# Modulation slabs in rounded pieces, with roots and forget sums made ahead of the local attentions

## What is computed

```python
q, k = rms_norm(q_heads, q_gain), rms_norm(k_heads, k_gain)   # fox and moba, heads of 64
c = cumsum(log_sigmoid(f + f_bias))                           # fox alone: forget sums
s = q @ k.T * d ** -0.5 + c[:, None] - c[None, :]             # then a causal softmax, times v
# moba: q and k are turned by a partial rope instead; no forget sums
...
# second block, needed there long after: a condition c and one for the context
mod_lat = jax.nn.silu(c) @ w_mod + b_mod                      # 1024 x 6144
mod_ctx = jax.nn.silu(c_ctx) @ w_mod + b_mod
```

## Time and profile before

| | us |
|---|---|
| Median of 3 runs (lowest, highest) | 2408.41 (2407.76, 2408.49) |
| The profiled execution's own time | 2396.61 |
| Its span in the profile | 2394.8 |
| Attention stage of layer 0, of layer 1 | 117.95, 117.95 |

### The profile page before, as it was taken

How to read it: one execution, slowest core, us unless ns; L and a number is a source line. 1 busy time by engine, 2 the same in 40 slices (tenths; PEclk the granted TensorE clock), 3 DMA queues, 4 the chain that set the end, 5 groups by cost and what they waited for, 6 DMA issues and landing times. The chain is left out here.

```text
span 2394.8 us, 41799 instructions
## 1 busy us (share of the span) xinstructions
PE 2197.3 (92%) x17910; PEld 1977.9 (83%) x17910; DVE 1003.1 (42%) x2016; ACT 1159.0 (48%) x1663; POOL 1205.6 (50%) x308
## 2 busy tenths in 40 slices
PE   8999989899999999889899999888978777998998
PEld 7999865489999999865488999766857777998998
DVE  2332754424222222565334221376656777333551
ACT  5544532466345434632356443555874554554443
POOL 6776610075878877630074876432310000675785
PEclk9999999899999999999999999898998988999999
DMA  7555422253556555431243655321213111553553
GB/s 258 169 170 171 154 72 89 70 176 123 194 171 200 185 176 180 141 123 64 97 141 111 199 180 172 114 70 53 72 58 103 37 34 40 192 170 127 176 179 115
DMA packets 304102, 319.02 MB, mean 133 GB/s; under 512 B 7897, under 2 KB 295117, under 8 KB 303405
## 3 DMA queue, kind: packets, MB, share of 16 engines
q1 hardware_dynamic: 303917, 316.34, 41.3%
HBM read 313.10 MB, written 3.21 MB: 132 GB/s over the span
## 5 line engine op out<-in xcount | busy, mean ns | idle before, releaser
L558 POOL TENSOR_TENSOR slab_lo<-ring,slab_hi 128x2048 fp32r<-128x2048 f32 (+2 forms) x188 | 843.5, 4499 | 560.0 <-ACT slab_hi L549 560.0
L549 ACT CAST slab_hi<-ring 128x2048 fp32r<-128x2048 f32 (+2 forms) x188 | 347.6, 1851 | 412.6 <-PE bank L449 284.9
L444 PE MATMUL bank<-x_parts_hi,slab_hi 128*128 128x256 f32 x1760 | 436.4, 286 | 0.5 <-ACT slab_hi L549 0.5
L445 PE MATMUL bank<-x_parts_lo,slab_hi 128*128 128x256 f32 x1760 | 431.6, 283 | 0.0
L444 PEld LDWEIGHTS bank<-x_parts_hi,slab_hi 128*128 128x128 f32 x1760 | 337.4, 192 | 3.8 <-issue 2.6
L445 PEld LDWEIGHTS bank<-x_parts_lo,slab_hi 128*128 128x128 f32 x1760 | 337.5, 192 | 1.2 <-issue 1.0
L379 POOL TENSOR_TENSOR slab_lo<-ring,slab_hi 128x2048 fp32r<-128x2048 f32 (+1 forms) x54 | 243.7, 4538 | 127.4 <-ACT slab_hi L368 91.9
L449 PE MATMUL bank<-x_parts_hi,slab_lo 128*128 128x256 f32 x1760 | 247.8, 283 | 7.8 <-POOL slab_lo L558 7.8
L449 PEld LDWEIGHTS bank<-x_parts_hi,slab_lo 128*128 128x128 f32 x1760 | 226.9, 192 | 9.4 <-POOL slab_lo L558 9.4
L411 PE MATMUL bank<-hidden_hi,slab_hi 128*128 128x256 f32 x704 | 194.4, 276 | 0.0
L412 PE MATMUL bank<-hidden_lo,slab_hi 128*128 128x256 f32 x704 | 194.3, 276 | 0.0
(11 more groups left out here) (659 smaller groups left out, 4972.2 us busy)
## 6 DMA issues: line engine op xcount, KB each, us to landing
ring<-in_ffn_w_in SPq DMA_DIRECT2D x88, 1024.0 KB, 5.1
ring<-in_ffn_w_out SPq DMA_DIRECT2D x32, 1024.0 KB, 5.1
ring<-in_w_in SPq DMA_DIRECT2D x27, 1024.0 KB, 5.3
ring<-in_mix_w_in SPq DMA_DIRECT2D x24, 1024.0 KB, 5.3
ring<-in_w_mod SPq DMA_DIRECT2D x24, 1024.0 KB, 5.1
ring<-in_w_up SPq DMA_DIRECT2D x22, 1024.0 KB, 5.1
ring<-in_ffn_w_out SPq DMA_DIRECT2D x16, 768.0 KB, 4.4
ring<-in_mix_w_out SPq DMA_DIRECT2D x8, 1024.0 KB, 5.2
```

Source lines behind the costliest of these rows:

```text
L444: pe.matmul(out, w[0][:, k, col], act[0][:, k, :], start=(k == 0), stop=False)
L445: pe.matmul(out, w[0][:, k, col], act[1][:, k, :], start=False, stop=False)
L549: act.copy(self.hi[p][:, 0:w], K.ring[n % RING][:, 0:w]).then_inc(self.hi_ready, 1)
L558: pool.tensor_tensor(self.lo[p][:, 0:w], place[:, 0:w], self.hi[p][:, 0:w].bitcast(F32), ALU.subtract)\
```

## The change

In the attention stage a modulation slab is taken in four pieces (128 partitions by two groups of 256). ACT rounds a piece (`act_round`), DVE makes its remainder (`dve_rest`), and PE multiplies both with four columns: the two conditions' rounded parts and their remainders (`c`). Four rows come out instead of two, and the last turn adds them with a selector (`sel`). There are three places for pieces. PE takes a piece at two of the loop's three calls a step, 36 in 18 steps, and none ahead of the loop. Squares, head sums and roots for q and k move into the inverse stage (`LocalRoots`), with one of the first three slabs ahead of them; the forget sums move into the projection (`ForgetSums`). The scan runs two steps ahead of the loop instead of four, the state's memset and first answer come behind the normed tiles on DVE, and the two rotations stand before the scan's second step.

```diff
@@ project_stage, act @@
                 last.then_inc(lora_read, 1)
+                act.wait_ge(forget_in, 1)
+                act.activation(forget.e, forget.e, ACT.Exp).then_inc(forget_exp, 1)
                 evacuate(12)
@@ project_stage, dve @@
+                own.after(dve, last)
+                forget.dve_bounded(dve, s["f"], col("f_bias")).then_inc(forget_in, 1)
                 heads(11)
+                dve.wait_ge(forget_exp, 1)
+                forget.dve_sums(dve)
                 heads(12)
+class ForgetSums:
...
+    def dve_bounded(self, dve, f, bias):
+        self.K.dve_own.after(dve, dve.tensor_scalar(self.x, f[:, :], bias[0:4, :], None, ALU.add))
+        return dve.scalar_tensor_tensor(self.e, self.x, -1.0, self.x, ALU.mult, ALU.min)
+    def dve_sums(self, dve):
+        own.after(dve, softplus_small(dve, own, self.e, self.s, self.s2, self.q, self.s))
...
+class LocalRoots:
+    BANK = 4
...
+    def act_squares(self, act):
+        for i in range(4):
+            act.activation(self.sq[:, 2 * i:2 * i + 2, :], self.qk[:, 2 * i:2 * i + 2, :], ACT.Square).then_inc(self.squared, 1)
+    def pe(self, pe):
+        for i in range(4):
+            pe.wait_ge(self.squared, i + 1)
+            pe.matmul(self.K.bank[self.BANK + i][:, :], self.K.c("headsum"),
...
+    def act_roots(self, act):
+        for i in range(4):
+            act.wait_ge(self.summed, i + 1)
+            last = act.activation(self.sq[:, 2 * i:2 * i + 2, :], K.bank[self.BANK + i][:, :].rearrange("p (a t) -> p a t", a=2),
+                                  ACT.Ln, bias=K.c("eps"), scale=1.0 / 64)
+            last.then_inc(self.logged, 1)
+        act.wait_ge(self.logged, 4)
+        act.activation(self.sq[:, :, :], self.sq[:, :, :], ACT.Exp, scale=-0.5)
@@ rwkv_stage @@
+                    pe.wait_ge(intra_read, 9)
+                    mod.pe_first(pe, 0, 1)
                     pe.wait_ge(intra_read, 16)
-                    mod.pe_first(pe)
+                    roots.pe(pe)
+                    mod.pe_first(pe, 1, mod.FIRST)
+                    roots.pe_free(pe)
                     inv.pe(pe)
...
-                    inv.act(act, between=lambda i: mod.act_first(act) if i == 1 else None)
+                    roots.act_squares(act)
+                    for g in range(4):
+                        inv.diagonal(act, g)
+                    roots.act_roots(act)
+                    inv.act(act, between=lambda i: mod.act_first(act) if i == 1 else None, first=4)
@@ Modulations @@
-    AT_A_CALL = 2
-    AHEAD = 8
+    CHUNKS = 4
+    PLACES = 3
...
+    def dve_c(self, dve):
+        dve.tensor_tensor(self.sel[:, :], K.c("ident", slice(0, 4), n=2), K.c("ident", slice(0, 4), first=2, n=2), ALU.add)
+        dve.wait_ge(self.c_hi, 1)
+        dve.tensor_tensor(self.c[:, :, 2:4], K.cs[:, :, :], self.c[:, :, 0:2].bitcast(F32), ALU.subtract).then_inc(self.c_lo, 1)
...
+    def act_round(self, act, upto):
+        for j in range(self.rounded, min(upto, self.end)):
+            n = self.n0 + self.FIRST + j // self.CHUNKS
+            act.wait_ge(K.loaded[n % RING].sem, K.landed[n])
+            if j >= self.PLACES:
+                act.wait_ge(self.used, j - self.PLACES + 1)
+            act.copy(self.hi[j % self.PLACES][:, :], self.piece(j)).then_inc(self.hi_ready, 1)
...
+    def dve_rest(self, dve, upto):
+        for j in range(self.rested, min(upto, self.end)):
+            dve.wait_ge(self.hi_ready, j + 1)
+            dve.tensor_tensor(self.lo[j % self.PLACES][:, :], self.piece(j), self.hi[j % self.PLACES][:, :].bitcast(F32),
+                              ALU.subtract).then_inc(self.lo_ready, 1)
...
+    def pe_chunks(self, pe, count):
+        for j in range(self.multiplied, min(self.multiplied + count, self.end)):
...
+            pe.wait_ge(self.lo_ready, j + 1)
+            out = K.bank[self.BANKS[n % 2]][0:4, 0:HALF]
+            for i, w in enumerate((view(self.hi[j % self.PLACES], per), view(self.lo[j % self.PLACES], per))):
+                for k in range(per):
+                    last = pe.matmul(out, self.c[:, part * per + k, :], w[:, k, :], start=(part == 0 and i == 0 and k == 0),
+                                     stop=(part == self.CHUNKS - 1 and i == 1 and k == per - 1))
...
+            last.then_inc(self.used, 1)
+    def act_copies(self, act, upto):
+        for n in range(self.copies, min(MOD_SLABS, self.FIRST + upto)):
+            act.wait_ge(self.used, self.CHUNKS * (n - self.FIRST + 1))
+            act.copy(self.rows[:, n * HALF:(n + 1) * HALF], K.bank[self.BANKS[n % 2]][0:4, 0:HALF]).then_inc(self.copied, 1)
...
     def pe_end(self, pe):
         pe.wait_ge(self.copied, MOD_SLABS)
         for t in range(2 * MOD_SLABS):
+            if t < 2 * self.FIRST:
+                pe.transpose(out, rows[0:2, :], K.c("ident", slice(0, 2), n=2))
+            else:
+                last = pe.matmul(out, rows, self.sel[:, :], start=True, stop=True)
@@ Attention.dve @@
                 self.dve_normed(dve, i - 1)
+            late(i)
@@ attention_stage @@
-        EARLY = 4
+        EARLY, ROT_BANKS = 2, (6, 3)
...
                 scan.pe(pe, 0)
+                pe.wait_ge(normed, 8)
                 for i in range(2):
...
+                scan.pe(pe, 1)
+                def mid_step(i):
+                    if i == 1:
+                        pe.wait_ge(roped, 2)
+                    scan.pe(pe, i + EARLY)
+                calls = iter(range(1000))
+                att.pe(pe, between=lambda: mod.pe_chunks(pe, 1 if next(calls) % 3 != 1 else 0), mid_step=mid_step)
...
+                mod.act_c(act)
+                mod.act_round(act, 2)
+                def at_step(i):
+                    mod.act_copies(act, max(0, 2 * i - 2) // mod.CHUNKS)
+                    mod.act_round(act, 2 * i + 4)
+                    scan.act(act, i + EARLY - 1)
...
+                def at_step(i):
+                    scan.dve(dve, i + EARLY - 1)
+                    if i < 2:
+                        rope(i)
+                scan.dve(dve, 0)
+                mod.dve_rest(dve, 2)
+                att.dve(dve, at_step=at_step, normed_first=True, late=lambda i: mod.dve_rest(dve, 2 * i + 4))
+                mod.dve_rest(dve, mod.end)
+                for step in range(len(units) + EARLY, scan.GATE + 4):
+                    scan.dve(dve, step)
                 mod.dve(dve)
```

More of the change, by code:

```diff
@@ L1887, in rwkv_stage @@
         mod = Modulations(K, ctx)
+        roots = LocalRoots(K, ctx)
         with ExitStack() as ictx:
@@ L1932, in _ @@
                     inv.pool(pool)
-        attention_stage(K, lt, xt, unit, mod)
+        attention_stage(K, lt, xt, unit, mod, roots.sq)
 class RwkvScan:
@@ L2144, in act_first, with act_c @@
         for n in range(self.FIRST):
-            act.copy(self.rows[:, n * HALF:(n + 1) * HALF], self.first_place(n)).then_inc(self.copied, 1)
+            act.copy(self.rows[0:2, n * HALF:(n + 1) * HALF], self.first_place(n)).then_inc(self.copied, 1)
         self.copies = self.FIRST
-    def some(self, pe):
+    def act_c(self, act):
+        act.copy(self.c[:, :, 0:2], self.K.cs[:, :, :]).then_inc(self.c_hi, 1)
+    def dve_c(self, dve):
         K = self.K
[L2150 to L2156, removed]
-                             start=(self.k == 0), stop=(self.k == KD - 1))
-            self.k += 1
-            if self.k == KD:
-                K.slab_done(last)
-                self.k, self.n = 0, self.n + 1
@@ L2163, in act @@
-    def act(self, act, step, calls):
-        K = self.K
-        while self.copies < min(MOD_SLABS, self.FIRST + (self.AHEAD + step * calls) * self.AT_A_CALL // KD):
-            n = self.copies
-            K.wait_slabs(act, self.n0 + n + 1)
-            act.copy(self.rows[:, n * HALF:(n + 1) * HALF], K.bank[self.BANKS[n % 2]][0:2, 0:HALF]).then_inc(self.copied, 1)
+        dve.tensor_tensor(self.sel[:, :], K.c("ident", slice(0, 4), n=2), K.c("ident", slice(0, 4), first=2, n=2), ALU.add)
+        dve.wait_ge(self.c_hi, 1)
@@ new lines, in dve_rest @@
+    def dve_rest(self, dve, upto):
[3 more added lines that the diff above has]
+                              ALU.subtract).then_inc(self.lo_ready, 1)
+            self.rested = j + 1
+    def pe_chunks(self, pe, count):
+        K, per = self.K, KD // self.CHUNKS
+        for j in range(self.multiplied, min(self.multiplied + count, self.end)):
+            n, part = self.FIRST + j // self.CHUNKS, j % self.CHUNKS
+            if j == 0:
+                pe.wait_ge(self.c_lo, 1)
+            if part == 0:
+                K.eaten += 1
+                pe.wait_ge(self.copied, max(self.FIRST, n - 1))
+            pe.wait_ge(self.lo_ready, j + 1)
[4 more added lines that the diff above has]
+                                     stop=(part == self.CHUNKS - 1 and i == 1 and k == per - 1))
+                    if part == self.CHUNKS - 1 and i == 0 and k == 0:
+                        K.slab_done(last)
+            last.then_inc(self.used, 1)
```

(12 more changed lines are left out.)

105 lines of the change are left out of this document (53 added, 52 removed).

## The result

The changed kernel takes 2426.9 us, the median of six executions (2416.4 to 2449.2), beside 2407.3 for the kernel before: a ratio of 1.0100, with an interval of 1.0069 to 1.0130. It is slower by 1.0%, where 2393.0 was forecast and 2380 to 2406 was the range. The profiled execution took 2430.5 us against 2396.6, which is 33.9 more, and in sum the two attention stages account for all of it: 129.14 and 140.71 us, together 269.85, where each had 117.95. That is 33.95 more.

The account below looks back on a forecast made before the run. PE was taken to set the pace in the loop's first ten steps, a dependency chain in the last eight; -9.2 in attention and +1.5 in the inverse stage gave -7.7 a layer, -15.4 for both: 2393.0 us, range 2380 to 2406.

Parts of the forecast that it names:

- Steps 0 to 9: First ten of 18 attention loop steps: 64.6 us become 57.1, saved 7.5 a layer, two new waits included.
- the wait for the rotated tiles: Loop step 1: PE waits until DVE has added both rotated tiles, 2.4 us.
- a colder stage: Rival: clock also falls at step 1's wait, tail and inverse chain dearer; 3.4 us a layer lost, 2401.6; chance 0.16.
- ACT and DVE become the chain: Rival, each loop step: a rounding and a remainder set the pace, 22.1 us a layer, 2437, half 2415; chance 0.12.
- dear pieces: Rival: a piece costs PE 0.95 us, so nothing is saved there; 13.7 us a layer, 2420; chance 0.06.
- the wait for y: Loop step 4: ACT's rounding, waiting for a place, stands ahead of the copy of y that PE wants, 1.1 us.
- A slab's product: PE in the attention loop: a rounded piece takes 0.57 us where a call of float32 products took 0.95.
- The opening: Attention stage until the first unit's scores: 27.2 us become 13.7, 2.2 of it for half clock; saved 13.5.
- Steps 10 to 17: Last eight attention loop steps: 23.2 us grow by 9.7, with 16 pieces, the mean and waits of 6.4.
- The end: Attention stage after the loop, until the modulations are turned: 3.0 us grow by 2.1 for last piece, copy and products.
- The inverse stage: It takes in the roots in ACT's 8.52 us hole; PE's 2.9 us wait lowers the clock, costing 1.5 a layer.
- The projection: It takes in DVE's 8.6 us of forget sums at no cost; 0.2 us to spare by the shared-port rule.

Follow-up runs that it names:

- e1: Changed kernel with the state's memset first on DVE and PE's wait for the rotated tiles moved ahead of the fifth piece: 2409.4 us, ratio 1.0010.
- e12: e1 with ACT's copy of y and the square for the variance put ahead of its two roundings of a step: 2370.1 us, ratio 0.9862.
- e14: Changed kernel with one line moved: ACT's copy of y and the square stand ahead of the roundings of their step: 2395.5 us, ratio 0.9970.
- e6: Changed kernel with every rounded matmul of a piece issued twice, the second into columns nobody reads: 2443.3 us, ratio 1.0125.
- e10: e1 with only the first three pieces of a layer rounded, the other 33 multiplying by these again: 2363.3 us, ratio 0.9820.
- e3: Changed kernel with float32 products in the pieces' places, no roundings or remainders, order and both waits kept: 2382.9 us, ratio 0.9939.
- e9: e7 with ACT still rounding every piece and DVE still forming every remainder, which nobody multiplies by: 2377.1 us, ratio 0.9880.
- e5: Changed kernel with the condition's parts repeated to 64 columns of weights in place of 4: 2443.9 us, ratio 1.0161.
- e11: e1 with every rounded matmul issued twice: 2406.5 us over all ten executions, ratio 0.9994.
- e7: e3 with the two waits taken away (memset first, rotated tiles' wait ahead of the fifth piece): 2360.6 us, ratio 0.9814.
- e13: e12 with the first two of the nine slabs as float32 products straight from the ring: 2367.3 us, ratio 0.9856.
- e8: e1 with 64 columns of weights in place of 4: 2411.9 us over all ten executions, 2379.1 to 2437.6, ratio 0.9945.

## Why the prediction was wrong

The step that failed is *Steps 0 to 9*: its two new waits were priced at their own lengths (2.4 and 1.1, together 3.5), and nothing was put for the clock, behind them or anywhere else in the loop. Measured were 1.86 and 1.25, and some 44 us at half clock in the first layer: a mean of 0.71 over 75.78 us is 58% of them at half. The windows above show 23.5 of them behind the wait for the rotated tiles, 3.5 behind the one for y, and 15.8 from 426 on with no wait ahead. In the second layer it is 24 us behind the rotated tiles (1126 to 1150) and 48 behind y. At full clock the first layer's 44 would be 22, and the stretch 53.8, an estimate from these rows. So the rest of the step was right or better.

The rival "a colder stage" had the mechanism and put it at 2.2 us for the wait in step 1, which kept its time inside the stated range; the 0.13 for a slower kernel was the chain's and the dear pieces'. That price took from the earlier trace rows how long a fall lasts, 5.2 us, and those are float32 slab products. In the attention loop a fall lasted from 378.7 to about 402, and behind the wait for y in the second layer for 48 us. The kernel before had a longer fall too, and in this very stage: behind the root's wait of 5.31 us it is at half from 457.88 to 474. One window of it:

```profile
456.00:472.00 16.00, 12.04 (x51) 7.80 (x52) 8.63 (x27) 5.99 (x22) 0.00 (x0) 0.50 0.01 2
```

The carry-over from one stage's products to another's is the error.

The wait for y was named and sized (1.1, measured 1.25) and treated as the smaller one. That ACT's order decides most of the loop's clock is shown by e1 against e12 and the changed kernel against e14, which differ in that order alone. That it does so through the wait for y is argued from the place: the changed kernel's second layer, e1's first and e6's second fall within some 2 us behind that wait, and e10, e12 and e14, which don't have it, don't fall there. The swap shortened the wait before the variance too (1.77 to 0.46 in e14); that one comes at the loop's end, behind the stretches compared here.

The other steps. *A slab's product*: 0.57, measured 0.56; "dear pieces" is out. *The opening*: 13.7, measured 16.05; the wait was 3.15 and the half clock lasted some 11 us instead of 4.5, the same error in small. *Steps 10 to 17*: 32.9, measured 31.74. *The end*: 5.1, measured 5.57. *The inverse stage*: PE waits 3.46 us for X and the clock falls to 0.62 over the next 4 us, as forecast, but attention starts at 352.79 against 352.83: the term of 1.5 was nothing, probably because ACT and DVE set that chain. The roots end at 334.79 on ACT, ahead of the 336.37 at which it is wanted next. *The projection*: no cost, by a narrow margin. DVE's first forget instruction behind the exponential, beside GpSimd's remainder:

```profile
300.45 4.62 POOL L558 TENSOR_TENSOR slab_lo<-ring,slab_hi 128x2048 fp32r<-128x2048 f32 x1 [6.21 <-ACT slab_hi L549]
...
301.68 3.54 DVE L2444 TENSOR_SCALAR h<-h 4x256 f32<-4x256 f32 x1 [2.57 <-ACT h L1499]
305.25 1.74 DVE L2445 RECIPROCAL h<-h 4x256 f32<-4x256 f32 x1
...
313.50 0.67 DVE L1526 TENSOR_TENSOR qk<-bank,rstd 128x512 f32<-128x512 f32 x1
```

An instruction that takes 0.28 us elsewhere on this shape took 3.54 and ended at 305.22; GpSimd's, 4.62 us from 300.45, ended at 305.07. The last norm ended at 314.17, and ACT's last copy at 314.54. By the Trainium skill ("SBUF — State Buffer", section "SBUF: two separate sides") the loser of the shared port pair waits for the other's whole instruction. The trace agrees with it, and the last norm came 0.2 us ahead of the 314.4 worked out by that rule. *ACT and DVE become the chain*: not as priced, for PE has hardly a wait beyond those listed; yet ACT's order did the harm, by the clock.

Left open: why rounded pieces and the wait of 1.25 us together hold the clock at half for over 40 us of unbroken work, where with float32 products it came back in some 16 (e3), and stayed at 1.00 beside the same roundings and behind a wait of 0.82 for y (e9). No experiment has float32 products behind a wait of 1.25 us for y. The number of weight columns (e5), PE's time in the products (e6, e11) and the roundings (e10) don't explain it alone. The fall without a wait, at 426 in the changed kernel and near 367 in e1, e10 and e12, is unexplained too. In each of these it begins within the state products on lines 2054 and 2057 of a scan step, but in e1's second layer, at 1131.3, within those on lines 2074 and 2075. With float32 products around them and no wait ahead it did not come (e7, e9, e13).

## What to carry to other kernels

Price a new wait of the engine that sets the pace by the clock of the work behind it, not by its length alone, and take how long a fall lasts from rows of the same stage and the same kind of products; where there are none, let the range hold half clock for the whole stretch. On an engine that feeds the critical one, put what is wanted now ahead of what prefetches, above all where the prefetch itself waits for a place. And undo one part at a time before judging a change: here the moves alone gave 0.9963, the changed kernel's order with float32 products 0.9939, and that without its two waits 0.9814; the rounded pieces in the order they came with were the loss (1.0100).

## What the runs showed of the hardware

PE's granted clock fell to half in the midst of matmuls without a gap, 15 us behind the last wait (e1: 14.78 us busy of 14.78 at 1.00, then 19.29 of 19.29 at 0.50). The same instructions in the same kernel ended 58 us apart with the clock (e8), where e7, at 1.00 through both stages, stays within 4 us. Of the waits, 3.0 to 3.5 us (the memset's) halved it in every profiled layer that had them, 1.25 us (for y) in some and not in others (e6), and 0.42 us was followed by a fall in one layer and not in the other (e3). Doubled work can cost less than its time: in the profiled executions e6's first layer, with twice the rounded matmuls, kept 1.00 through the loop and took 124.0 us (353.18 to 477.20) where the changed kernel's took 129.1.
